# Two parts of h as one 512-column moving operand, with main and cross halves added when a bank is emptied

## What is computed

```python
for i in range(2):
    h = rmsnorm(x, norm_mix[i])
    if i == 0:
        bg, cg, xv = split(h @ a_w_in, 3)
        x = x + (bg * causal_dwconv(cg * xv, a_conv)) @ a_w_out
    else:
        q = h @ b_w_q                      # 8 heads of 128
        x = x + attention(q, k, v) @ b_w_o # causal, ALiBi; one block of 256 keys
    g, u = split(rmsnorm(x, norm_ffn[i]) @ w_up[i], 2)    # 2816 columns each
    x = x + (silu(causal_dwconv(g, w_conv[i]) + b_conv[i]) * u) @ w_down[i]
    if i == 0:
        k, v = split(rmsnorm(x, kv_norm) @ w_kv, 2)
out = rmsnorm(x, final_norm)
```

## Time and profile before

| | |
|---|---|
| runs | 601.89 us median (601.01 to 602.15) |
| profiled execution | span 600.3 us between first and last instruction; about 1.6 us of the median lie around it |
| TensorE matmul | 591.0 us busy, 98% of the span, 4239 matmuls |
| VectorE | 386.3 us, 64% |
| ScalarE | 288.4 us, 48% |
| DMA | 108.02 MB, 180 GB/s |
| granted TensorE clock | 0.998 of full over the span |

### The profile page before, as it was taken

How to read it: one execution, slowest core, us unless ns; L and a number is a source line. 1 busy time by engine, 2 the same in 40 slices (tenths; PEclk the granted TensorE clock), 3 DMA queues, 4 the chain that set the end, 5 groups by cost and what they waited for, 6 DMA issues and landing times.

```text
span 600.3 us, 10234 instructions
## 1 busy us (share of the span) xinstructions
PE 591.0 (98%) x4239; PEld 558.0 (93%) x4239; DVE 386.3 (64%) x450; ACT 288.4 (48%) x325; POOL 10.5 (2%) x22
## 2 busy tenths in 40 slices
PE   8999999999999999999999999999999999999995
PEld 6999998999999999999899999889999999999994
DVE  4686767576555656567786677785666655655554
ACT  5534353565543554445455455644754443454431
POOL 2000000000000000000100000000000000000001
PEclk9999999999999999999999999999999999999999
DMA  8996466356664555655656544353565665554001
GB/s 276 344 297 204 159 235 218 115 194 211 211 199 156 199 162 193 208 160 192 211 158 216 189 141 141 141 210 106 170 233 164 206 210 163 186 175 174 0 1 70
DMA packets 80912, 108.02 MB, mean 180 GB/s; under 512 B 1833, under 2 KB 71665, under 8 KB 80882
## 3 DMA queue, kind: packets, MB, share of 16 engines
q1 hardware_dynamic: 80160, 104.97, 53.1%
q10 hardware_dynamic: 722, 2.63, 1.2%
HBM read 106.54 MB, written 1.05 MB: 179 GB/s over the span
## 4 chain that ended last, share of the span: by engine, by line
PE 95%; DMA 1%; DVE 1%; issue 1%; ACT 1%; POOLq 0%; POOL 0%; SPq 0%; DVEq 0%; ACTq 0%
PE proj L784 22%; PE proj L786 22%; PE proj L785 22%; PE acc L826 8%; PE acc L828 8%; PE acc L830 8%; PE tr L840 1%; PE acc L786 1%; PE acc L785 1%; PE acc L784 1%; DMA xs<-in_x 1%; PE tr L785 1%; PE tr L786 1%; PE tr L784 1%; PE tr L889 0%
## 5 line engine op out<-in xcount | busy, mean ns | idle before, releaser
L522 DVE TENSOR_TENSOR w_lo<-raw,w_hi 128x2048 fp32r<-128x2048 f32 x94 | 215.1, 2292 | 84.7 <-ACT w_hi L324 83.4
L784 PE MATMUL proj<-hA_hi,w_hi 128*128 128x256 f32 x864 | 245.0, 284 | 0.0
L786 PE MATMUL proj<-hA_hi,w_lo 128*128 128x256 f32 x864 | 244.6, 283 | 0.0
L785 PE MATMUL proj<-hA_lo,w_hi 128*128 128x256 f32 x864 | 244.5, 283 | 0.0
L324 ACT ACTIVATE w_hi<-raw 128x2048 fp32r<-128x2048 f32 x94 | 179.4, 1909 | 53.3 <-PE acc L830 41.1
L784 PEld LDWEIGHTS proj<-hA_hi,w_hi 128*128 128x128 f32 x864 | 165.8, 192 | 0.7
L785 PEld LDWEIGHTS proj<-hA_lo,w_hi 128*128 128x128 f32 x864 | 165.8, 192 | 0.7
L786 PEld LDWEIGHTS proj<-hA_hi,w_lo 128*128 128x128 f32 x864 | 165.8, 192 | 0.0
L609 DVE SCALAR_TENSOR_TENSOR scratch<-proj,f_par,scratch 128x255 f32<-128x255 f32 (+1 forms) x80 | 33.1, 476 | 48.2 <-ACT scratch L391 48.2
L391 ACT ACTIVATE scratch<-proj,f_par 128x256 f32<-128x256 f32 x40 | 20.4, 559 | 69.7 <-PE proj L786 69.7
L826 PE MATMUL acc<-w_hi,kq_hi 128*128 128x512 f32 x160 | 49.6, 391 | 0.0
(11 more groups left out here) (127 smaller groups left out, 661.5 us busy)
## 6 DMA issues: line engine op xcount, KB each, us to landing
raw<-in_ffn_w_up SPq DMA_DIRECT2D x44, 1024.0 KB, 5.1
raw<-in_ffn_w_down SPq DMA_DIRECT2D x22, 1024.0 KB, 4.9
raw<-in_a_w_in SPq DMA_DIRECT2D x11, 1024.0 KB, 10.8
raw<-in_w_kv SPq DMA_DIRECT2D x8, 1024.0 KB, 5.3
raw<-in_a_w_out SPq DMA_DIRECT2D x4, 1024.0 KB, 4.8
raw<-in_b_w_q SPq DMA_DIRECT2D x4, 1024.0 KB, 5.2
raw<-in_b_w_o SPq DMA_DIRECT2D x4, 1024.0 KB, 4.9
raw<-in_a_w_in SPq DMA_DIRECT2D x2, 512.0 KB, 7.8
```

What stands on the lines that cost most here:

```text
L522: dve.tensor_tensor(wlo, raw[:, s % RAW, :], whi.bitcast(F32), ALU.subtract).then_inc(w_lo_ready, 2 if s + 1 in AHEAD else 1)
L784: pe.matmul(dst, sh, mh, start=first, stop=False)
L785: pe.matmul(dst, sh, ml, start=False, stop=False)
L786: return pe.matmul(dst, sl, mh, start=False, stop=last)
```

## The change

- **One operand.** The hi and lo parts of h lie in one tensor (`hA[:, 2, KD, S]`). `project` issues two matmuls for each k, not three: weight hi against 512 moving columns (h hi, then h lo) into a whole bank, and weight lo against 256 columns (h hi) into its first half. A wide slot now fills two banks (`pair[b]`); of each, the first half is the "main" sum and the second the "cross" sum.
- **Adding.** The two halves are added when the banks are emptied: ScalarE copies the cross halves to SBUF (`whole`, `a_whole`), VectorE adds the main halves. TensorE waits for that sum (`f_sum`, `a_sum`, `kq_sum`) where it waited for the bank's reader. There are now no `proj` and `tr` banks of their own; the four banks of the pairs serve for all.
- **Openings two at once.** `rows_of_two` streams two slots as 512 columns. It needs both from the start. V's last two slots are done so too. The turned openings go to `acc[0]`.
- **Order.** The down rows of unit j-2, not j-1, come with unit j; four units for each turn of the loop, not two, and four act buffers. In the attention, weighing moves into the next pair's K slot; scores move behind that slot; transposes of the probabilities behind the whole Q slot. Heads use `acc[1]` (the last pair uses `pair[0]`).

```diff
@@ TensorE: project, rows of two, openings
             def project(s, b, hid, e):
                 whi, wlo = split_slot(s)
+                dst = pair[b][:, e, :]
                 for k in range(KD):
                     w = slice(256 * k + P * e, 256 * k + P * e + P)
-                    last = split_matmul(bank[b][:, 256 * e:256 * e + S],
-                                        ((whi[:, w], wlo[:, w]), (hid[0][:, k, :], hid[1][:, k, :])),
-                                        k == 0, k == KD - 1)
+                    pe.matmul(dst.rearrange("p (a n) -> p a n", a=2), whi[:, w], hid[:, :, k, :], start=k == 0, stop=False)
+                    last = pe.matmul(dst[:, 0:S], wlo[:, w], hid[:, 0, k, :], start=False, stop=k == KD - 1)
                 return last
+            def rows_of_two(s, t, n=None, late=None):
...
+                for k in range(KD):
+                    if late and k == KD - 2:
+                        late()
+                    if n is not None and k % 4 == 0:
+                        pe.wait_ge(h_lo_ready, step4(n, t, k // 4))
+                    w = slice(256 * k, 256 * k + 256)
+                    last = split_matmul(by_rows[t].rearrange("p (s n) -> p s n", s=2),
+                                        ((hA[:, 0, k, tok], hA[:, 1, k, tok]),
+                                         (wgt[:, 0, a:b + 1:b - a, w], wgt[:, 1, a:b + 1:b - a, w])),
+                                        k == 0, k == KD - 1)
+            def open_two(s, n):
+                wait_slot(s)
+                wait_slot(s + 1)
+                rows_of_two(s, 0, n, lambda: transposes(n, 1)).then_inc(rows_done, 1)
+                rows_of_two(s, 1, n).then_inc(slot_done, 2)
@@ TensorE: V and attention
+            open_two(V0, 2)
+            wait_slot(V0 + 2)
+            wait_slot(V0 + 3)
+            pe.wait_ge(v_lo_ready, 1)
+            rows_of_two(V0 + 2, 0).then_inc(rows_done, 1)
+            transposes(3, 0)
+            pe.wait_ge(v_lo_ready, 2)
+            rows_of_two(V0 + 2, 1).then_inc(slot_done, 2)
+            transposes(3, 1)
...
             for p in range(NH // 2 - 1):
                 sK, sQ = KQ0 + 2 * p + 2, KQ0 + 2 * p + 3
                 wait_slot(sK)
-                pe.wait_ge(kq_lo_ready, 2 * p + 1)
-                project(sK, 0, hidA, 0)
+                pe.wait_ge(kq_sum, 2 * p + 1)
+                project(sK, 0, hA, 0)
+                if p:
+                    weigh(2 * p - 2)
+                    weigh(2 * p - 1)
+                project(sK, 0, hA, 1).then_inc(slot_done, 1)
                 scores(2 * p)
                 scores(2 * p + 1)
-                project(sK, 0, hidA, 1).then_inc(slot_done, 1)
-                wait_slot(sQ)
-                project(sQ, 1, hidB, 0)
+                pe.wait_ge(kq_sum, 2 * p + 2)
+                wide_slot(sQ, 1, hB)
                 transpose_probs(2 * p)
                 transpose_probs(2 * p + 1)
-                project(sQ, 1, hidB, 1).then_inc(slot_done, 1)
-                weigh(2 * p)
-                weigh(2 * p + 1)
...
+            out_rows_of(0, 0)
+            weigh(2 * p - 2)
+            weigh(2 * p - 1)
             scores(2 * p)
             scores(2 * p + 1)
@@ ScalarE: V, attention
+            hi(V0 + 3)
+            v(0, 0)
+            v(0, 1)
...
+            for p in range(NH // 2 - 1):
+                if p:
+                    heads_mixed(p - 1)
+                kq_copy(2 * p + 2)
                 exp(2 * p)
                 exp(2 * p + 1)
+                hi(KQ0 + 2 * p + 5)
+                kq(2 * p + 2)
+                kq_copy(2 * p + 3)
+                kq(2 * p + 3)
+                heads_probs(p)
+                if p < NH // 2 - 2:
+                    hi(KQ0 + 2 * p + 6)
+            hi_ahead(2)
+            heads_mixed(NH // 2 - 2)
@@ VectorE: V, attention
             lo(V0 + 2)
+            lo(V0 + 3)
+            v(0, 0)
+            normalise(3, 0)
+            v(0, 1)
...
+            for p in range(NH // 2 - 1):
+                if p:
+                    heads_mixed(p - 1)
+                kq_whole(2 * p + 2)
+                row_max(2 * p)
+                row_max(2 * p + 1)
+                normal_probs(2 * p)
+                normal_probs(2 * p + 1)
+                lo(KQ0 + 2 * p + 5)
+                kq(2 * p + 2)
+                kq_whole(2 * p + 3)
+                kq(2 * p + 3)
+                heads_probs(p)
+                if p < NH // 2 - 2:
+                    lo(KQ0 + 2 * p + 6)
+            lo_ahead(2)
+            heads_mixed(NH // 2 - 2)
@@ VectorE: the FFN's unit
+                if j >= 3:
+                    lo(s + 2, turn)
+                dve.wait_ge(f_cross, after(f_turn(l, j, 0), turn, 2 * LOOPED))
+                dve.tensor_tensor(whole[:, 0], whole[:, 0], main[0], ALU.add).then_inc(f_sum, 1)
+                lo(s + 3, turn)
+                taps(l, j, whole[:, 0], turn)
+                dve.wait_ge(f_cross, after(f_turn(l, j, 1), turn, 2 * LOOPED))
+                dve.tensor_tensor(whole[:, 1], whole[:, 1], main[1], ALU.add).then_inc(f_sum, 1)
+                dve.wait_ge(f_sum, after(f_turn(l, j, 1), turn, 2 * LOOPED))
+                glued(l, j, whole[:, 1], turn)
+                lo(s + 4, turn)
+                acts(l, j, turn)
```

More of the change, by code:

```diff
@@ L166, in build @@
         c_copied = sem("c_copied")
+        a_cross = sem("a_cross")
+        a_sum = sem("a_sum")
         cx_ready = sem("cx_ready")
@@ L407, in ffn @@
                 with act.Fori(0, TURNS) as turn:
-                    unit(l, 1, turn)
-                    unit(l, 2, turn)
-                unit(l, UNITS - 2)
+                    for j in range(3, 3 + LOOPED):
+                        unit(l, j, turn)
                 if l == 0:
                     hi_ahead(1)
-                unit(l, UNITS - 1)
+                    hi(V0)
             def exp(h):
@@ new lines, in _, with heads_probs @@
+            v(0, 0)
+            v(0, 1)
+            hi(KQ0)
+            v(1, 0)
+            for h in range(2):
+                h_hi(3, 0, h)
+            v(1, 1)
+            for h in range(2):
+                h_hi(3, 1, h)
+            load_gain(4)
+            hi(KQ0 + 1)
+            hi(KQ0 + 2)
+            kq_copy(0)
+            hi(KQ0 + 3)
+            kq(0)
+            kq_copy(1)
+            kq(1)
+            hi(KQ0 + 4)
+            def heads_probs(p):
+                for e in range(2):
+                    act.wait_ge(probs_T, 2 * p + e + 1)
+                    act.activation(pt_hi[:, e, :], head_bank(2 * p + e)[:, 0:384], ACT.Copy).then_inc(pt_hi_ready, 1)
@@ L605, in unit @@
                         if back == 2:
[L606 to L607 removed]
+                            dve.wait_ge(conv_op, after(4 * U + e + 1, turn, 4 * LOOPED))
+                        f = after(2 * j + e, turn, 2 * LOOPED)
                         dst = g[:, e, back:S]
[L609 removed]
+                        dve.scalar_tensor_tensor(out=dst, in0=gate[:, e, 0:S - back],
@@ L629, in ffn @@
+            def ffn(l):
+                s = FFN[l]
+                lo(s + 2)
+                lo(s + 3)
+                lo(s + 4)
+                taps(l, 0, acc[0][0][:].rearrange("p (e n) -> p e n", e=2))
+                dve.wait_ge(opening_T, 2 * (l + 1) + 2)
+                glued(l, 0, acc[0][1][:].rearrange("p (e n) -> p e n", e=2))
+                acts(l, 0)
+                unit(l, 1)
+                unit(l, 2)
                 with dve.Fori(0, TURNS) as turn:
-                    unit(l, 1, turn)
@@ L631, in ffn, with a_whole_sum @@
-                    unit(l, 2, turn)
-                unit(l, UNITS - 2)
+                    for j in range(3, 3 + LOOPED):
+                        unit(l, j, turn)
                 if l == 0:
                     lo_ahead(1)
-                unit(l, UNITS - 1)
+                    lo(V0)
+            def a_whole_sum(i, b):
+                dve.wait_ge(a_cross, a_turn(i, b))
+                dve.tensor_tensor(a_whole[:, b], a_whole[:, b], main[b], ALU.add).then_inc(a_sum, 1)
+            c_all, cx = a_whole[:, 0], a_whole[:, 1]
@@ L775, in _ @@
+            lo_ahead(2)
+            heads_mixed(NH // 2 - 2)
+            row_max(NH - 2)
+            row_max(NH - 1)
+            normal_probs(NH - 2)
+            normal_probs(NH - 1)
+            lo(O0 + 2)
+            heads_probs(NH // 2 - 1)
+            lo(O0 + 3)
+            heads_mixed(NH // 2 - 1)
+            lo(FFN[1])
             boundary(2, 4)
```

613 lines of the change are left out of this document (319 added, 294 removed).

## The result

The changed kernel takes 604.88 us (median of four runs, 603.93 to 605.28), against 601.87 for the kernel before. The ratio is 1.005, 95% interval 1.0036 to 1.0064: slower by half a percent, where 598.1 and "faster" were forecast.

What follows compares the result with a forecast made beforehand. TensorE's matmul stream was taken to bound the kernel: gains of 11.6 (projections) and 2.4 us (rows of two slots), less losses of 1.1, 6.3, 2.7 and 0.1, net 3.8 off 601.9, gave 598.1 us; range 591.5 to 603.5.

Steps and rivals of the forecast that it cites:

- What bounds the kernel: Whole kernel: TensorE's stream of matmuls bounds it, with no stall to remove; only 12.5 ns per removed matmul can be won.
- Projections: All projection groups: two matmuls for each k instead of three, 360 ns down to 347.5 per group, gain 11.6 us.
- 928 groups: Count of projection groups, 58 slots of 16, each given the full 12.5 ns gain.
- My bounds of 320 and 360 for the group: Projection group in ns: 320 if only columns counted, 360 if the second run cost a matmul of its own; 347.5 taken.
- The rule against this: All matmuls: the skill's 2.5 ns gap per matmul would make the whole gain 2.8 us, against 14.0 in the sum.
- Work beside TensorE: Copies on ScalarE and additions on VectorE for wide slots: loops cost nothing; 0.1 us late at the first FFN's end.
- V and the heads: V's last two slots and the attention heads: TensorE stalls of 1.1 us, 6.3 us and 2.7 us.
- The three stalls: TensorE waits: v_lo in V 1.1 us, pt_lo in three head pairs 6.3, mix_lo before the last scores 2.7.
- The sum: Whole kernel: gain 14.0 us less loss 10.2 us, net 3.8 us, giving 598.1 us.
- Rival 4: Heads: hand-overs between ScalarE and VectorE take longer; 1.3 us more each gives 602.0, 2 us gives 604; chance 0.14.
- the walk: Step-by-step timing of the engines' queues through FFN, V and heads, from which waits were forecast; total 598.1 us.

Runs made afterwards that it cites:

- the way back: The changed kernel with project issuing three matmuls again for k = 1 to 7, k = 0 keeping its 512 columns: 610.56 us.
- The order experiment: The changed kernel with ScalarE's and VectorE's work at the heads reordered and the last pair's scores no longer waiting for mix_lo: 592.06 us.

## Why the prediction was wrong

Two terms of the sum were mis-sized: the stalls were priced at their own length, without the lower clock that came with them (4.6 us), and all 928 groups were given a gain that 512 of them did not have in full (3.4 us with the down rows).

- **What bounds the kernel.** This was right. TensorE's stream did, and the gain was to be read from distances between starts.
- **Projections.** The price was right outside the loop: 12.9 ns per group in mixer A, 0.348 us in units 1 and 2, and the way back costs it again (610.56). The step that failed is "928 groups": in the 512 groups of the loop's units the gain was 7 ns and not 12.5, a miss of 3.4 us with the down rows. The cause of this slower rhythm stays open. I had no row of 512 and 256 columns in turn and took the two distances as if neither minded its neighbour. My bounds of 320 and 360 for the group held.
- **The rule against this.** By the gap that the Trainium skill gives ("TensorE: Matmul & The Clock Gate", "Back-to-back issue gap") the gain would have been 2.8 us. That section gives it for an isolated matmul, which the prediction left out, and says that in a stream with weight loads the loads help to set the spacing; here every matmul has its own load. The trace decides: mixer A alone gained 2.1 us and the two FFNs 6.3, and the 12.5 ns of the earlier trace rows came back in mixer A as 12.9.
- **Work beside TensorE.** It was right to cost the loops at nothing; no matmul waited for a sum anywhere.
- **V and the heads.** The three stalls were found and sized: 1.1, 6.3 and 2.7 forecast, 1.0, 5.5 and 2.5 by the wait records. (Between a pair's last matmul before weighing and the weighing the starts leave 2.0 us, nearer to my 2.1.) The order experiment took those of the heads away; that of V, 1.0 us, stayed.
- **The sum.** This is the step that failed in the heads: a stall was priced at its own length. The clock fell during one wait and just after another, and the work done at the lower level took 4.6 us longer, on top of 9 us of waiting. I had no rival for it. TensorE waited nowhere between 16 us and its last matmul, and its clock was full in every stretch I read. But the trace before has one fall that I had not read. TensorE's last matmul starts at 593.19, and with nothing after it the clock is full up to 598 and then falls:

```profile
594.00:598.00 4.00, 0.00 (x0) 0.00 (x0) 2.66 (x7) 0.72 (x2) 0.93 (x1) 1.00 0.01 2
598.00:600.00 2.00, 0.00 (x0) 0.00 (x0) 0.00 (x0) 0.00 (x0) 0.00 (x0) 0.56 0.70 262
```

  That TensorE's standing still can take the clock down was there to see; that waits of 2 us can do it was not.
- **The rivals.** Rival 4, with 602 to 604, came nearest in time, for the wrong reason: the hand-overs took no longer than walked. With the term for the clock and the loop's units at 0.353 the walk gives 598.1 + 4.6 + 3.4 = 606.1; 604.9 were measured. In the span of the profiled run the same sum gives 4.2 us more than before, where 2.6 were measured: 1.2 us of the difference are the earlier start of A's wide slots, and most of the rest is that the FFNs lost 2.8 us and not 3.4. This is an account after the fact; which waits would take the clock down no row of the kernel before could tell.

## What to carry to other kernels

A stall of TensorE, where TensorE bounds a kernel, costs more than its length if the clock falls with it; a change that brings the first 2 us waits into a stream without any should be priced both ways. When work is added beside the bounding engine, look at the order of the queue that the hand-over passes through, not only at its load: here the same work on VectorE and ScalarE in another order, with one wait of TensorE dropped, brought 12.8 us. And a price per instruction read from runs of one kind need not hold when two kinds alternate.

## What was not expected of the hardware

- The granted clock went to half with two of four waits of about 2 us at the heads: after the first, some 0.7 us after TensorE had gone back to work, and during the fourth, for nearly 7 us, 2.9 us of which were lost. Filling the waits with useless matmuls kept it full and won 3.9 us.
- 512 and 256 columns in turn have two rhythms, 0.348 and 0.353 us for the same pair of matmuls at the same clock. Which one holds depends on what came just before, and two or three matmuls of 128 columns change it to the faster.
- A moving operand of two runs of 256 columns, 8 KB apart, with the following 256 columns takes 0.348 us in the faster rhythm, no more than 0.2275 for one run of 512 and 0.120 for one of 256. In the timeline the starts are 0.23 and 0.12 us apart in turn.
